# Earlier halves, moved waits, and small products placed between the halves of projection units

## The chip, the cores and the metric

The kernel runs on one core of one Trainium2 chip. The metric is the device time of one execution in microseconds, as the median of the runs shown. Five engines run their own instruction queues in order and meet at semaphores: TensorE (PE, matrix products), VectorE (DVE), ScalarE (ACT), GpSimd (POOL) and SyncE (SP, which issues the loads).

## What is computed

x is 256 tokens by 1024, in fp32. Four layers follow each other. The first two have a token mixer and a feed-forward part, with a layer norm after each; the second of them feeds forward through eight experts, two per token. The last two are of another kind:

```python
def token_mixer(x, ...):                       # first block, both layers
    q_a, k_a, v_a, x_m, z_m = split(x @ w_in)
    y_a = dilated_attention(q_a, k_a, v_a, rel_bias)
    y_m = sigmoid(z_m) * norm(mlstm(conv(x_m), x_m))
    g_a, g_m = split(sigmoid(x @ w_gate + b_gate))
    return (g_a * (y_a @ w_br_a) + g_m * (y_m @ w_br_m)) @ w_o
...
for l in range(DEPTH):                         # second block
    p = rms_norm(x) @ w_in[l]
    y_a = conformer_conv(p)                    # 31 taps over 256 channels, layer norm, silu
    y_b = head_rms_norm(moba_attention(p))     # 4 heads of 64; with 256 tokens plain causal attention
    y_c = head_rms_norm(gla_chunked(p)) * silu(p)   # 4 heads, chunks of 32, a state carried between them
    x = x + concatenate([y_a, y_b, y_c]) @ w_out[l]
    x = x + conv_swiglu(rms_norm(x))
return rms_norm(x)
```

## The kernel before

Every weight comes in units of 1 MB (128 partitions by 2048 fp32 numbers), in one order for the whole program. SP loads unit u into one of six `raw` slots when the unit six earlier has been split. ACT copies it rounded to `w_hi` and DVE writes the rest to `w_lo` (`split`, L1329 and L1738); both have three slots, so ACT waits until PE has used the unit three earlier. PE makes each product as three (`product`, L626 to L628: high by high, high by low, low by high). Activations are split in the same way (`xT_hi`, `xT_lo`).

The order on each engine is written out by hand, with `ahead(n)` for the split of unit n + 2 of the second mixer. In what follows "the low part" is DVE's half of a split. A projection unit is 48 products of 128x256; `project_tok` and `project_T` can run a function `between` their halves of 24.

- Start: ACT splits units 0 and 1, then copies the transposed x in four quarters (`x_parts`); DVE has the low parts behind it. POOL reads the shifted relative bias back from memory and loads small tables.
- First mixer's end: the gated branches are merged quarter by quarter on DVE (L2065, L2067), ACT copies them and DVE writes the low part (`low`, L2036). Five output units (`WO_UNITS`) use them; `busy_while_norm` then keeps PE at dummy products until the norm's diagonals `dg` allow `transpose_x`.
- Router and experts: DVE ranks the logits, writes `pick` (which token sits in which slot) and `extra_ready`; PE gathers the tokens (`dispatch`) and runs 14 steps per expert, each with two units up and one down. After the last expert its output is split (`expert_out`: `eo_hi`, `eo_lo`), scattered to tokens by four pairs of products, weighted into x and normed.
- Second mixer (`mixer2`, twice): units 0 to 10 are projections, 11 to 14 outputs (`w_out`). Between them stand small products: `within_chunks`, `state_steps`, `gla_out` (the memory's four heads, 36 products of 128 columns), `scores` and the attention heads (`next_pair`). 18 of the 31 taps of the convolution run on POOL, 13 on DVE (`convolve`). DVE carries the state over eight chunks in `st8` (L2330).

In the second mixer PE's order after unit 7 was:

```python
pe.wait_ge(S_.state_ready, L + 1)
gla_out((0,))
pe.wait_ge(S_.proj2_out, L * 11 + 8)
scores(0, (2, 3))
scores(1, (4, 7))
gla_out((1, 2, 3))
tok(8)
```

## Time and profile before

| what | us |
|---|---|
| median of 3 runs (2372.72 to 2376.57) | 2374.25 |
| the profiled execution | 2371.58 |
| its span, first to last instruction | 2369.8 |
| PE busy in the span | 2298.3 |
| DVE busy | 1734.5 |
| ACT busy | 1346.8 |

The span is what the trace covers; the profiled execution has 1.8 us more around it. PE is busy 97% of the span, so an idle time elsewhere matters only where PE ends up waiting for it. PE's products overlap, and their ends are modelled, so a busy PE is not always a fast one: its granted clock stands beside it.

### The profile page before, as it was taken

To read this page: it belongs to the slowest core of one execution; us is meant where nothing else is said; L and a number is where in the kernel's file an instruction comes from. 1 tells how busy PE (TensorE), PEld (TensorE's weight loads), DVE (VectorE), ACT (ScalarE), POOL (GpSimd) and SP (SyncE) were. 2 spreads that over 40 slices of the span, in tenths; PEclk is the share of its full clock that TensorE was granted. 3 is DMA by queue.
4 is the path that set the end of the run, shared out by engine and by line. 5 is a ranking of instruction groups with operands and counts; after the bars stand their busy time and mean duration, and the time that the engine had idled before them with its cause. 6 is when DMAs were issued, how large, how long until landed. Compare 5 with 4: busy or idle time off the path is not lost.

```text
span 2369.8 us, 41753 instructions
## 1 busy us (share of the span) xinstructions
PE 2298.3 (97%) x16557; PEld 2154.3 (91%) x16557; DVE 1734.5 (73%) x1853; ACT 1346.8 (57%) x1346; POOL 186.7 (8%) x181
## 2 busy tenths in 40 slices
PE   7999999999899999999999999999889999999998
PEld 7999999999799999999999999999888999898997
DVE  4556555557588888888888888888566777676776
ACT  4643433554376767676767776776336444636443
POOL 2000000100000000000000000000390000670000
PEclk9999999999999999999999999999979999999999
DMA  9344655534399999999999999999432555433551
GB/s 301 116 143 145 211 177 177 175 108 152 121 357 335 354 339 350 335 353 333 357 350 337 347 337 351 335 350 344 126 107 90 179 176 195 129 116 118 202 174 56
DMA packets 423083, 554.41 MB, mean 234 GB/s; under 512 B 9907, under 2 KB 377253, under 8 KB 422993
## 3 DMA queue, kind: packets, MB, share of 16 engines
q1 hardware_dynamic: 419232, 544.85, 68.2%
q0 software_dynamic: 3760, 8.31, 1.3%
q8 instruction: 62, 1.02, 0.2%
q14 instruction: 29, 0.23, 0.0%
HBM read 552.06 MB, written 1.06 MB: 233 GB/s over the span
## 4 chain that ended last, share of the span: by engine, by line
PE 86%; DVE 6%; ACT 3%; DVEq 2%; issue 1%; DMA 1%; ACTq 0%; SPq 0%
PE ps L626 26%; PE ps L627 26%; PE ps L628 26%; DVE w_lo L1738 2%; ACT w_hi L1329 2%; PE ps L1008 1%; PE ps L671 1%; PE ps L1025 1%; PE ps L1204 1%; DVE cvT L2238 1%; DVEq L2239 0%; DMA raw<-in_w_in 0%; PE ps L824 0%; PE ps L1202 0%; PE ps L1070 0%
## 5 line engine op out<-in xcount | busy, mean ns | idle before, releaser
L1738 DVE TENSOR_TENSOR w_lo<-raw,w_hi 128x2048 fp32r<-128x2048 f32 x519 | 1181.5, 2286 | 338.2 <-ACT w_hi L1329 336.5
L1329 ACT ACTIVATE w_hi<-raw 128x2048 fp32r<-128x2048 f32 x519 | 986.5, 1907 | 252.2 <-PE ps L628 232.1
L626 PE MATMUL ps<-w_hi,xg_hi 128*128 128x256 f32 x1792 | 516.8, 288 | 2.2 <-DVE w_lo L1738 2.2
L628 PE MATMUL ps<-w_hi,xg_lo 128*128 128x256 f32 x1792 | 504.9, 282 | 0.0
L627 PE MATMUL ps<-w_lo,xg_hi 128*128 128x256 f32 x1792 | 504.8, 282 | 0.0
L626 PE MATMUL ps<-xT_hi,w_hi 128*128 128x256 f32 (+1 forms) x1712 | 490.1, 286 | 11.0 <-DVE xT_lo L1748 6.8
L627 PE MATMUL ps<-xT_lo,w_hi 128*128 128x256 f32 (+1 forms) x1712 | 485.8, 284 | 0.0
L628 PE MATMUL ps<-xT_hi,w_lo 128*128 128x256 f32 (+1 forms) x1712 | 485.7, 284 | 0.0
L626 PEld LDWEIGHTS ps<-w_hi,xg_hi 128*128 128x128 f32 x1792 | 338.1, 189 | 9.4 <-DVE xg_lo L2150 2.9
L626 PEld LDWEIGHTS ps<-xT_hi,w_hi 128*128 128x128 f32 (+1 forms) x1712 | 328.4, 192 | 16.1 <-issue 8.9
L627 PEld LDWEIGHTS ps<-w_lo,xg_hi 128*128 128x128 f32 x1792 | 338.3, 189 | 3.8
L628 PEld LDWEIGHTS ps<-w_hi,xg_lo 128*128 128x128 f32 x1792 | 338.0, 189 | 0.0
L627 PEld LDWEIGHTS ps<-xT_lo,w_hi 128*128 128x128 f32 (+1 forms) x1712 | 328.5, 192 | 1.6
L628 PEld LDWEIGHTS ps<-xT_hi,w_lo 128*128 128x128 f32 (+1 forms) x1712 | 328.3, 192 | 0.4
L626 PE MATMUL ps<-w_hi,hT_hi 128*128 128x512 f32 x536 | 212.7, 397 | 1.0 <-DVE hT_lo L2159 1.0
L627 PE MATMUL ps<-w_lo,hT_hi 128*128 128x512 f32 x536 | 212.0, 395 | 0.0
L628 PE MATMUL ps<-w_hi,hT_lo 128*128 128x512 f32 x536 | 211.6, 395 | 0.0
L626 PE MATMUL ps<-w_hi,xT_hi 128*128 128x256 f32 (+1 forms) x448 | 130.9, 292 | 9.1 <-DVE w_lo L1738 5.5
L627 PE MATMUL ps<-w_lo,xT_hi 128*128 128x256 f32 (+1 forms) x448 | 128.7, 287 | 0.0
L628 PE MATMUL ps<-w_hi,xT_lo 128*128 128x256 f32 (+1 forms) x448 | 128.7, 287 | 0.0
L628 PEld LDWEIGHTS ps<-w_hi,hT_lo 128*128 128x128 f32 x536 | 100.8, 188 | 23.8
L1551 ACT ACTIVATE sa<-ps 128x256 f32<-128x256 f32 x112 | 43.1, 385 | 139.3 <-PE ps L628 139.1
(455 smaller groups left out, 2840.2 us busy)
## 6 DMA issues: line engine op xcount, KB each, us to landing
raw<-in_exp_w SPq DMA_DIRECT2D x336, 1024.0 KB, 5.8
raw<-in_ffn_w_up SPq DMA_DIRECT2D x44, 1024.0 KB, 5.1
raw<-in_w_in SPq DMA_DIRECT2D x42, 1024.0 KB, 6.2
raw<-in_ffn_w SPq DMA_DIRECT2D x33, 1024.0 KB, 5.1
raw<-in_ffn_w_down SPq DMA_DIRECT2D x22, 1024.0 KB, 5.5
raw<-in_w_gate SPq DMA_DIRECT2D x16, 1024.0 KB, 5.4
raw<-in_w_out SPq DMA_DIRECT2D x8, 1024.0 KB, 4.9
raw<-in_w_o SPq DMA_DIRECT2D x6, 1024.0 KB, 5.8
```

The lines of the kernel that those rows point to most:

```text
L626: pe.matmul(out, lhs[0], rhs[0], start=first, stop=False)
L627: pe.matmul(out, lhs[0], rhs[1], start=False, stop=False)
L628: return pe.matmul(out, lhs[1], rhs[0], start=False, stop=last)
L671: m = pe.matmul(o[:, c, t, :], piece, dg[:, t, :], start=True, stop=True)
L1008: m = pe.matmul(bank(0, KC, P)[:, k, :], x[:, t, k * P:(k + 1) * P], pick[:, t, :], start=t == 0, stop=t == TT - 1)
L1025: m = pe.transpose(ps[:, 7, c * P:(c + 1) * P], hf[:, 0, c * P:(c + 1) * P], ident)
L1204: m = pe.matmul(o, qgm[rows, h // 2, t, j, :], st8[rows, 4 * t + j, h // 2, :], start=False, stop=j == 3)
L1329: act.activation(w_hi[:, u.const % SPL, 0:width], raw[:, u.const % RAW, 0:width], ACT.Copy)\
L1551: act.activation(sa[:, odd, 0:FFC], ps[:, 6, 0:FFC], ACT.Silu).then_inc(S_.silue_ready, 1)
L1738: dve.tensor_tensor(w_lo[:, u.const % SPL, 0:width], raw[:, u.const % RAW, 0:width], w_hi[:, u.const % SPL, 0:width].bitcast(F32), ALU.sub ...
L2238: dve.scalar_tensor_tensor(cvT[:, c, :], avT[:, c, k:k + S], w, cvT[:, c, :], ALU.mult, ALU.add)
```

## The change

It changes orders and waits; PE's products stay the same but for 30 dummies.

- Start: unit 0 is loaded, split and used in two halves, behind the first two and the last two quarters of x; the constants are loaded after unit 3, and POOL's read of the bias waits for unit 3, the loads behind it for the convolution.
- First mixer's end: `low(0)` and `low(1)` stand together after the first pair; PE does the first halves of output units 0 and 1, then the second halves; unit 1's second tile sums in bank 4.
- Router: the split of unit 2 moves from before the ranking to after `pick`; the gates move behind step 1.
- Last expert: the output is summed, split, scattered and added half by half, in the norm's order. 120 dummies in place of 90 before the second block.
- Second mixer: PE's scores go between the halves of unit 8, two heads of `gla_out` after it, two between the halves of unit 9; the second attention pair and the first gated transposes between the halves of unit 10; the sums over channels between the halves of output units 0 and 1; output rows 3 before 1. DVE and ACT are reordered to match; unit 5's split goes ahead of the gate's logarithm.

```diff
-SUM_BANKS = ((0, 5), (1, 1), (2, 2), (3, 3), (4, 4))
+SUM_BANKS = ((0, 5), (1, 4), (2, 2), (3, 3), (4, 4))
...
-OUT2_ROWS = (2, 1, 3, 0)
-OUT2_BANKS = (1, 2, 4, 5)
+OUT2_ROWS = (2, 3, 1, 0)
+OUT2_BANKS = (1, 2, 5, 6)
...
-            sp.dma_start(cst_init[:], A["const3"]).then_inc(S_.start_loaded, 16)
-            sp.dma_start(cst1[:], A["const1"]).then_inc(S_.start_loaded, 16)
...
                 for n, c in enumerate(IN1_COLS):
+                    if (L, n) == (0, 0):
+                        for half in range(2):
+                            k = slice(4 * half, 4 * half + 4)
+                            sp.dma_start(raw[:, 0, :].rearrange("p (k n) -> p k n", k=KC)[:, k, :], columns(w_in, 256 * c, 256)[:, k, :])\
+                              .then_inc(raw_landed[0] if half else S_.half_landed, 16)
+                        continue
                     load(u + n, columns(w_in, 256 * c, 256), UW, c == 0)
+                    if (L, n) == (0, 3):
+                        sp.dma_start(cst_init[:], A["const3"]).then_inc(S_.start_loaded, 16)
+                        sp.dma_start(cst1[:], A["const1"]).then_inc(S_.start_loaded, 16)
...
-            pool.dma_start(shifted[:], bass.AP(tensor=bias_rows.tensor, offset=0, ap=[[1, P], [BUCKET_W, HA], [1, S]]))\
-                .then_inc(S_.bias_loaded, 16)
...
+                else:
+                    pool.wait_ge(raw_landed[3], 16)
+                    pool.dma_start(shifted[:], bass.AP(tensor=bias_rows.tensor, offset=0, ap=[[1, P], [BUCKET_W, HA], [1, S]]))\
+                        .then_inc(S_.bias_loaded, 16)
+                    pool.wait_ge(S_.conv1_done, 1)
                 pool.dma_start(norm_gb[:, 0, :], over(A["ln_g"][L, 0], D)).then_inc(S_.norm_loaded, 16)
...
+                if halves:
+                    pe.wait_ge(S_.lo_half, 1)
+                    w = [v[:, 0, :].rearrange("p (k n) -> p k n", k=KC) for v in (w_hi, w_lo)]
...
+                        if halves and (c, k) == (0, 4):
+                            pe.wait_ge(S_.lo_ready, RAW + 1)
...
+                def out_half(n, half, parts):
+                    c0, w = WO_UNITS[n]
+                    for t in range(TT):
+                        for k in range(4 * half, 4 * half + 4):
+                            m = product(bank(SUM_BANKS[n][t], TT, w)[:, t, :], [v[:, t * P:(t + 1) * P] for v in x_chunks[k]],
+                                        [v[:, k, :] for v in parts[n]], k == 0, k == KC - 1)
+                    if half:
+                        m.then_inc(S_.unit_used, 1)
+                pe.wait_ge(S_.xT_lo_ready, L * 12 + 6)
+                parts = [unit_parts(u + 22, KC, WO_UNITS[0][1])]
+                out_half(0, 0, parts)
+                parts.append(unit_parts(u + 23, KC, WO_UNITS[1][1]))
+                out_half(1, 0, parts)
+                pe.wait_ge(S_.xT_lo_ready, L * 12 + 8)
+                out_half(0, 1, parts)
+                out_half(1, 1, parts)
...
+                    for h in range(2):
+                        for c in range(2):
+                            m = product(ps[:, 4 + h, :], [v[:, 0, 0, c * P:(c + 1) * P] for v in (hT_hi, hT_lo)],
+                                        [v[:, c, h * HALF:(h + 1) * HALF] for v in w], False, c == 1)
+                        m.then_inc(S_.unit_used if h else S_.eo_psum, 1)
...
                 for q in range(4):
-                    scatter(q, q)
+                    if q % 2 == 0:
+                        pe.wait_ge(S_.eo_lo_ready, item.value(plus=2 + q // 2))
+                    scatter(NORM_ORDER[q], q)
...
-                busy_while_norm(6, 10 if L else 90)
+                busy_while_norm(6, 10 if L else 120)
...
-                gla_out((0,))
-                pe.wait_ge(S_.proj2_out, L * 11 + 8)
-                scores(0, (2, 3))
-                scores(1, (4, 7))
-                gla_out((1, 2, 3))
-                tok(8)
+                def both_scores():
+                    pe.wait_ge(S_.proj2_out, L * 11 + 8)
+                    scores(0, (2, 3))
+                    pe.wait_ge(S_.state_ready, L + 1)
+                    scores(1, (4, 7))
+                tok(8, both_scores)
+                gla_out((0, 1))
+                tok(9, lambda: gla_out((2, 3)))
                 next_pair = attention(L, HB, (sb0, sb1), pT2, vb, (S_.pT2_psum, S_.pT2_ready, S_.pv2), (2, 3),
                                       (ps[:, 4, 0:256], ps[:, 4, 256:512]))
                 pe.wait_ge(S_.expd2, L + 1)
                 next_pair(0)
...
-                def first_values():
+                def second_pair():
                     pe.wait_ge(S_.proj2_out, L * 11 + 9)
                     next_pair(1)
-                tok(9, first_values)
+                    gated_T(0)
+                tok(10, second_pair)
                 next_pair(2)
-                pe.wait_ge(S_.conv_ready, L + 1)
-                channel_sum(0, cvT, S_.csum_psum)
-                tok(10, lambda: gated_T(0))
-                def both_T():
+                def sum_and_T():
+                    pe.wait_ge(S_.conv_ready, L + 1)
+                    channel_sum(0, cvT, S_.csum_psum)
+                    gated_T(1)
+                def square_and_T():
                     attended_T()
-                    pe.wait_ge(S_.yT2_lo_ready, L * 4 + 1)
-                    gated_T(1)
+                    pe.wait_ge(S_.csq_ready, L + 1)
+                    channel_sum(S, agT, S_.cvar_psum)
                 bank_free(11)
-                w_out(0, yM_chunks[0:2], both_T)
-                pe.wait_ge(S_.csq_ready, L + 1)
-                channel_sum(S, agT, S_.cvar_psum)
-                w_out(1, yA_chunks[2:4])
-                w_out(2, yM_chunks[2:4])
+                w_out(0, yM_chunks[0:2], sum_and_T)
+                w_out(1, yM_chunks[2:4], square_and_T)
+                w_out(2, yA_chunks[2:4])
                 w_out(3, yA_chunks[0:2])
                 busy_while_norm(7, 10)
...
-                expert_out(at)
+                for h in range(2):
+                    if h == 0:
+                        act.wait_ge(S_.eo_psum, 1)
+                    else:
+                        used(at)
+                    act.activation(eo_hi[:, h * HALF:(h + 1) * HALF], ps[:, 4 + h, :], ACT.Copy).then_inc(S_.eo_hi_ready, 1)
...
+                ahead(3)
                 act.wait_ge(S_.glog_in, L + 1)
...
                 act.activation(egT[:], egT[:], ACT.Ln, bias=1.0).then_inc(S_.gln_ready, 1)
-                ahead(3)
                 out(3, kcT[:], bank(1, 2, S))
...
                     m.then_inc(S_.yT2_hi_ready, 1)
                 pT_pair(0)
-                ahead(9)
+                ahead(10)
                 pT_pair(1)
-                out(9, rt2[:, :, 0:256], bank(1, TT, 256), ACT.Silu)
-                ahead(10)
                 act.wait_ge(S_.yc_psum, L * 2 + 1)
-                high(yM_hi[:, 0:2, :], 3, 70)
+                high(yM_hi[:, 0:2, :], 7, 70)
+                out(10, rt2[:, :, 256:512], bank(0, TT, 256), ACT.Silu)
+                ahead(11)
+                act.wait_ge(S_.yc_psum, L * 2 + 2)
+                high(yM_hi[:, 2:4, :], 3, 72)
                 square_root(S_.sqrt2_in, S_.sqrt2_out, L * 3 + 2, stat[:, 112:120])
                 act.wait_ge(S_.cent_ready, L + 1)
                 act.activation(agT[:], cvT[:], ACT.Square).then_inc(S_.csq_ready, 1)
-                out(10, rt2[:, :, 256:512], bank(0, TT, 256), ACT.Silu)
-                ahead(11)
                 act.wait_ge(S_.yb_psum, L + 1)
                 high(yA_hi[:, 2:4, :], 0, 74)
-                act.wait_ge(S_.yc_psum, L * 2 + 2)
-                high(yM_hi[:, 2:4, :], 3, 72)
                 square_root(S_.sqrt2_in, S_.sqrt2_out, L * 3 + 3, agT[:, 0, :])
...
+                ahead(14)
                 square_roots(8 * L + 4)
                 x_parts(L * 8 + 20, 0, scale=gain(2 * L + 1))
-                ahead(14)
...
-                x_parts(L * 12, 4, beta(1) if L else None)
+                if L:
+                    x_parts(L * 12, 4, beta(1))
+                else:
+                    x_parts(0, 4, parts=(0, 1))
+                    first_half()
+                    x_parts(0, 4, parts=(2, 3))
+                    second_half()
                 split(u + 1)
...
-                            if b:
-                                low(b - 1)
+                            if b == 3:
+                                low(2)
+                        if c == 0:
+                            low(0)
+                            low(1)
...
-                split(Count(MOE_UNIT0 + 2))
-                dve.wait_ge(S_.lgT_psum, 1)
+                dve.wait_ge(S_.logits_psum, 2)
...
-                dve.wait_ge(S_.totals_psum, 1)
+                split(Count(MOE_UNIT0 + 2))
+                dve.wait_ge(S_.slots_psum, 2)
...
-                gates()
                 for j in range(1, EARLY):
                     step(Count(0), j, False)
+                    if j == 1:
+                        gates()
...
-                expert_out(item)
-                dve.wait_ge(S_.y_psum, item.value(4, 4))
-                for t in range(TT):
-                    dve.scalar_tensor_tensor(x[:, t, :], bank(2 * t, D), gate_of[:, t, bass.ds(item.value(), 1)], y_sum[:, t, :],
-                                             ALU.mult, ALU.add)
-                dve.drain()
-                for t, h in QUARTERS:
+                for h in range(2):
+                    dve.wait_ge(S_.eo_hi_ready, item.value(plus=1 + h))
+                    q = slice(h * HALF, (h + 1) * HALF)
+                    dve.tensor_tensor(eo_lo[:, q], ps[:, 4 + h, :], eo_hi[:, q].bitcast(F32), ALU.subtract).then_inc(S_.eo_lo_ready, 1)
+                for q, (t, h) in enumerate(NORM_ORDER):
+                    dve.wait_ge(S_.y_psum, item.value(4, q + 1))
+                    dve.scalar_tensor_tensor(quarter(t, h), ps[:, q, :], gate_of[:, t, bass.ds(item.value(), 1)],
+                                             y_sum[:, t, h * HALF:(h + 1) * HALF], ALU.mult, ALU.add)
+                    dve.drain()
                     half_stats(t, h)
...
                 m.then_inc(S_.glog_in, 1)
+                ahead(3)
...
                 ahead(6)
-                convolve(3)
-                ahead(7)
+                convolve(1)
...
                 m.then_inc(S_.state_ready, 1)
+                ahead(7)
+                convolve(2)
...
                 ahead(8)
+                convolve(CW - taps[0])
+                ahead(9)
...
                 gated(0)
+                dve.wait_ge(S_.conv_part_ready, L + 1)
+                dve.tensor_tensor(cvT[:], cvT[:], conv_part[:], ALU.add).then_inc(S_.conv_ready, 1)
                 ahead(10)
+                low(yM_lo[:, 0:2, :], 7, 70, yM_hi[:, 0:2, :], 1)
+                gated(1)
```

DVE at the start, before, from its last constants on (`w_lo` is the low part of a unit, `xT_lo` that of a quarter of x):

```order
L2459 MEMSET stat 128x1
L1738 TENSOR_TENSOR w_lo<-raw,w_hi 128x2048
L1925 MEMSET xmT 128x4x3
L1748 TENSOR_TENSOR xT_lo<-ps,xT_hi 128x512 x4
L1738 TENSOR_TENSOR w_lo<-raw,w_hi 128x2048 x3
L1899 TENSOR_SCALAR xcT<-xmT,cols 128x256 x4
```

and in the changed kernel:

```order
L2538 MEMSET stat 128x1
L1991 MEMSET xmT 128x4x3
L1814 TENSOR_TENSOR xT_lo<-ps,xT_hi 128x512 x2
L1802 TENSOR_TENSOR w_lo<-raw,w_hi 128x1024
L1814 TENSOR_TENSOR xT_lo<-ps,xT_hi 128x512 x2
L1808 TENSOR_TENSOR w_lo<-raw,w_hi 128x1024
L1792 TENSOR_TENSOR w_lo<-raw,w_hi 128x2048 x3
```

A whole unit stood before the four quarters; now half a unit follows each two of them.

DVE after the last expert's last unit, before (`eo_lo` the low part of its output, BN_STATS the norm's sums):

```order
L1738 TENSOR_TENSOR w_lo<-raw,w_hi 128x2048
L2164 ISA
L2165 TENSOR_TENSOR eo_lo<-ps,eo_hi 128x1024
L2213 ISA
L2215 ISA
L2215 SCALAR_TENSOR_TENSOR x<-ps,gate_of,y_sum 128x1024
L2215 ISA
L2215 SCALAR_TENSOR_TENSOR x<-ps,gate_of,y_sum 128x1024
L1865 BN_STATS stat<-x 128x6 x4
```

and in the changed kernel:

```order
L1792 TENSOR_TENSOR w_lo<-raw,w_hi 128x2048
L2289 ISA
L2291 TENSOR_TENSOR eo_lo<-ps,eo_hi 128x512
L2289 REGISTER_ALU
L2291 TENSOR_TENSOR eo_lo<-ps,eo_hi 128x512
L2293 ISA
L2294 ISA
L2294 SCALAR_TENSOR_TENSOR x<-ps,gate_of,y_sum 128x512
L1931 BN_STATS stat<-x 128x6
L2293 REGISTER_ALU
L2294 ISA
L2294 SCALAR_TENSOR_TENSOR x<-ps,gate_of,y_sum 128x512
```

The output and x are made in halves and quarters, and the statistics of a quarter follow it at once.

PE in layer 0's second mixer, before, from unit 7's last products (`kbT,qbT` are the scores, `vc,atT` and `st,qgm` the memory's heads):

```order
L627 MATMUL ps<-xT_lo,w_hi 128x256
L628 MATMUL ps<-xT_hi,w_lo 128x256
L1202 MATMUL ps<-vc,atT 128x128
L1204 MATMUL ps<-st,qgm 128x128 x3
L1202 MATMUL ps<-vc,atT 128x128
L1204 MATMUL ps<-st,qgm 128x128 x4
L1192 MATMUL ps<-kbT,qbT 128x128 x4
L1192 MATMUL ps<-kbT,qbT 128x256 x4
L1202 MATMUL ps<-vc,atT 128x128
L1204 MATMUL ps<-st,qgm 128x128 x3
```

and in the changed kernel, at the middle of unit 8:

```order
L635 MATMUL ps<-w_hi,xT_hi 128x256
L636 MATMUL ps<-w_lo,xT_hi 128x256
L637 MATMUL ps<-w_hi,xT_lo 128x256
L1225 MATMUL ps<-kbT,qbT 128x128 x4
L1225 MATMUL ps<-kbT,qbT 128x256 x4
L635 MATMUL ps<-w_hi,xT_hi 128x256
L636 MATMUL ps<-w_lo,xT_hi 128x256
```

and after unit 8, up to the first products of unit 9:

```order
L636 MATMUL ps<-w_lo,xT_hi 128x256
L637 MATMUL ps<-w_hi,xT_lo 128x256
L1235 MATMUL ps<-vc,atT 128x128
L1237 MATMUL ps<-st,qgm 128x128 x3
L1235 MATMUL ps<-vc,atT 128x128
L1237 MATMUL ps<-st,qgm 128x128 x4
L1235 MATMUL ps<-vc,atT 128x128
L1237 MATMUL ps<-st,qgm 128x128 x3
L1235 MATMUL ps<-vc,atT 128x128
L1237 MATMUL ps<-st,qgm 128x128 x4
L629 REGISTER_ALU
L635 MATMUL ps<-w_hi,xT_hi 128x256
```

The scores stood after the first head, with no unit between unit 7 and them; they now divide unit 8, and the first two heads lie between units 8 and 9.

## Rows read from the trace of the kernel before

**Rows 1.** Page: busy us (share, instructions); clock in 40 slices.

```profile
PE 2298.3 (97%) x16557; PEld 2154.3 (91%) x16557; DVE 1734.5 (73%) x1853; ACT 1346.8 (57%) x1346; POOL 186.7 (8%) x181
...
PEclk9999999999999999999999999999979999999999
```

**Rows 2.** PE's waits over the span: us in total, times, longest.

```profile
PE ps L626 <- DVE w_lo L1738: 12.0, 6, 3.3
PE ps L671 <- DVE dg L1846: 9.7, 4, 5.8
...
PE ps L1202 <- DVE st L2330: 5.2, 2, 3.5
```

**Rows 3.** Windows: length, busy us (instructions) by engine, PE clock, DMA, GB/s.

```profile
15.84:22.67 6.83, 4.21 (x20) 4.25 (x21) 5.21 (x7) 3.52 (x10) 6.83 (x9) 0.50 1.06 363
1683.97:1821.10 137.13, 129.80 (x884) 120.02 (x884) 88.20 (x160) 63.93 (x80) 77.81 (x67) 0.87 0.33 110
2027.98:2156.06 128.08, 121.70 (x884) 113.74 (x884) 91.68 (x160) 65.73 (x81) 80.29 (x68) 0.93 0.37 122
1750.84:1802.19 51.35, 46.93 (x277) 42.61 (x277) 28.70 (x84) 17.89 (x27) 24.50 (x22) 0.73 0.25 82
2097.73:2137.15 39.42, 36.84 (x277) 34.37 (x277) 28.45 (x79) 17.90 (x27) 20.53 (x19) 0.96 0.33 108
1753.22:1780.53 27.31, 26.16 (x104) 22.14 (x105) 11.09 (x33) 3.04 (x9) 22.12 (x20) 0.50 0.16 53
```

**Rows 4.** Timeline at the start, ACT, PE: start, us, instruction, idle before.

```profile
12.12 1.91 ACT L1329 ACTIVATE w_hi<-raw 128x2048 fp32r<-128x2048 f32 x1 [6.72 <-DMA raw<-in_w_in]
15.13 1.91 ACT L1329 ACTIVATE w_hi<-raw 128x2048 fp32r<-128x2048 f32 x1 [1.10 <-DMA raw<-in_w_in]
16.95 2.01 ACT L1347 ACTIVATE xT_hi<-ps 128x256 fp32r<-128x256 f32 x7
...
8.05 3.65 PE L669 MATMUL ps<-cst,x 128*128 128x128 f32 x16 [3.17 <-issue]
18.45 0.55 PE L626 MATMUL ps<-xT_hi,w_hi 128*128 128x256 f32 x1 [6.76 <-DVE xT_lo L1748]
```

**Rows 5.** Timeline at the output units of layer 0, DVE then PE.

```profile
182.01 0.69 DVE L2036 TENSOR_TENSOR xT_lo<-ga,xT_hi 128x512 fp32r<-128x512 f32 x1 [1.07 <-ACT xT_hi L1526]
...
186.18 0.69 DVE L2036 TENSOR_TENSOR xT_lo<-ga,xT_hi 128x512 fp32r<-128x512 f32 x1
...
187.01 0.36 PE L626 MATMUL ps<-w_hi,xT_hi 128*128 128x256 f32 x1 [1.81 <-DVE xT_lo L2036]
```

**Rows 6.** Timeline of PE in the first expert's second step.

```profile
649.18 0.39 PE L626 MATMUL ps<-w_hi,xg_hi 128*128 128x256 f32 x1 [2.17 <-DVE w_lo L1738]
```

**Rows 7.** Timeline after the last expert, ACT, DVE, then PE.

```profile
1661.18 1.02 ACT L1560 ACTIVATE eo_hi<-ps 128x1024 fp32r<-128x1024 f32 x1 [1.88 <-PE ps L628]
...
1667.00 2.48 DVE L2215 SCALAR_TENSOR_TENSOR x<-ps,gate_of,y_sum 128x1024 f32<-128x1024 f32 x2 [3.54 <-PE ps L1071]
1669.55 2.47 DVE L1865 BATCH_NORM_STATS2 stat<-x 128x6 f32<-128x512 f32 x4
...
1682.95 0.16 DVE L1844 RECIPROCAL stat<-stat 128x1 f32<-128x1 f32 x1 [4.01 <-DMA cst<-in_const]
...
1666.64 11.49 PE L677 MATMUL ps<-yA_hi 128*128 128x256 f32 x90
```

**Rows 8.** Chain that ended last: transposes that open the second mixers.

```profile
1683.97 5.92 PE ps L671 x32
...
2027.98 3.84 PE ps L671 x32
```

**Rows 9.** Timeline of PE: unit 5, second channel sum, last output unit.

```profile
1725.14 0.38 PE L626 MATMUL ps<-w_hi,xT_hi 128*128 128x256 f32 x1 [2.21 <-DVE w_lo L1738]
...
1808.67 0.60 PE L1231 MATMUL ps<-agT,cst 128*128 128x256 f32 x2
...
1821.10 0.49 PE L626 MATMUL ps<-w_hi,yA_hi 128*128 128x512 f32 x1 [0.48 <-DVE yA_lo L2412]
```

101 lines of the change are left out of this document (52 added, 49 removed).

## The prediction

> **What bounds the kernel now.** I read the page first: PE is busy 2298.3 of 2369.8 us, and the clock line has one slice of the last third at 7 [rows 1]. So TensorE's queue is the length of the program, and only three things can shorten it, since the change keeps its work almost unchanged: time in which PE is idle (71.5 us), work done at the lower clock level (1.2 in place of 2.4 GHz), and the tail. Then PE's waits: the largest are for `w_lo`, for the diagonals `dg` of the norms, and for `st8` [rows 2]. Then windows over the stretches at the low clock and over the two second mixers [rows 3]. Those two windows hold the same 884 PE instructions, at mean clocks 0.87 and 0.93 and in 137.1 and 128.1 us; the reader is to see that layer 0 is 9 us slower for nothing in the code. Most of that lies in one part: from the end of unit 7 to the first output unit, 277 instructions took 51.35 us in layer 0 and 39.42 in layer 1, since 27.31 us of the former ran at clock 0.50 [rows 3]. The timeline gives the rest.
>
> **1. The start.** PE's first product begins at 18.45 us, after 6.76 us of idling for `xT_lo`: ACT takes units 0 and 1 (1.91 us each, from 12.12 and 15.13, as they land) before the transposed x, which PE had ready at 11.7 [rows 4]. In the new order ACT copies two quarters of x, half a unit, two quarters, half a unit. A unit of 1 MB takes 15.13 - 12.12 = 3.0 us to land, and the 832 columns of constants now behind four units were 832/2048 of one, 1.2 us. So half 0 lands at 12.1 - 1.2 - 1.5 = 9.4 us. ACT: x quarters to 10.1 (2.01/7 = 0.29 us per copy, two per quarter), half of 1.91 to 11.1. DVE: half of its unit's 2.3 us, to 12.3. PE starts at about 12.35, and its first 12 products, at the start's slow 0.21 us each (20 in 4.21 us, [rows 3]), cover quarters 2 and 3 and the second half, whose low part is there at 14.7. **-6.1 us.** Before, the slow clock held on for 4.2 us after the first product; I take the same again. Unit 1 must be split by 20.0: landed at 13.9, ACT to 15.8, DVE to 18.1. POOL's copy of `shifted` now waits for unit 3 (about 22 us), and nine small loads behind it for the convolution (about 33); the norm needs them after 200 us, `shifted` is needed at 41. Only what is left ahead of it, `wqk` (0.8 MB, 2.3 us of the queues), can push units 1 and 2, with 2 and 4 us of room. Bounds: -4 (a late unit 1) to -8 (the clock rises early).
>
> **2. The output units, twice.** PE waits 1.81 us for `low(1)`, which DVE writes behind a split and a gating, at 186.18 [rows 5]. Written straight after `low(0)` (182.0) it ends at 183.4, before PE needs it (185.2). The second wait, for `low(3)`, moves from about 189.6 to 189.9, but PE now has the first halves of two units, 48 products (5.8 us, to 191.0), in place of 24. After that both queues are as before. 2 x 1.81: **-3.6 us**; bounds -3.6 and -2.
>
> **3. Router and first expert.** The split taken off the router's front (2.3 us) comes back between `pick` and `extra_ready`, and PE dispatches only after `extra_ready`: no gain. The gates no longer stand ahead of unit 3's split; PE's 2.17 us wait for it goes [rows 6]. But the gates' 2.7 us now come after step 1: DVE reaches the split of the next step's gating half about 0.9 us after PE could start it. **-1.3 us**; bounds -2.2 and 0.
>
> **4. The last expert and the norm after it.** Before: `eo_hi` whole (1.02), `eo_lo`, four scatters, then DVE 2.48 for x and 2.47 for the statistics, to 1672.0 [rows 7]. Now the first half is copied while PE does the second; DVE is held by its split to 1661.6, then does two halves of 0.65 to 1662.9; PE scatters from 1662.4; DVE starts on the first quarter at 1663.1 and needs 4 x (0.69 + 0.69) = 5.5 us, to 1668.6. **-3.4 us**, and all behind it follows: the norm, the load of `cst2`, which is issued after the norm and is what DVE waits for (4.01 us at 1682.95, [rows 7]); the new order leaves that wait alone. PE's idle 5.83 us before the transposes (the 9.7 of [rows 2] holds it) is covered by 30 more dummies: 120 at 11.49/90 = 0.128 us are 15.3 us, from 1664.8 to 1680.1, against `dg` at 1683.9 - 3.4 = 1680.5. So they don't delay the transposes, by only 0.4 us, and the clock should not fall: the 32 transposes took 5.92 us here and 3.84 in layer 1 [rows 8]. **-2.1 us.** Bounds for both: -6 and -3.
>
> **5. The second mixers.** PE's instructions are the same, only placed elsewhere. A mean clock of 0.87 means 0.13/0.5 x 137.13 = 35.7 us at half speed, which cost 17.8; in layer 1 17.9 us cost 9.0. So the work at full clock is 129.8 - 17.8 = 112.0 and 121.7 - 9.0 = 112.7: take 112.5 [rows 3]. To it comes what PE still waits for. I followed the new queues with durations of the same instructions:
> - Unit 5's split before the log: its waits of 2.21 us [rows 9] and, in layer 1, 3.3 [rows 2] go, and ACT and DVE are 1.7 us earlier. But PE now meets what was hidden behind unit 5: `within_chunks` needs `qkg_ready`, 1.8 us after unit 5, and unit 6 its split, 0.4 us.
> - The state steps (5.2 us of waits, [rows 2]) end at about 1748 in layer 0's clock, PE asks for them at 1752: hidden behind unit 7 and the first half of unit 8. The scores need unit 7's copy, 0.7 us after PE's end of it; hidden too.
> - Unit 9 around `gla_out` leaves ACT waiting for unit 9 with the root and the transposed heads queued behind it. The heads' values are wanted by PE after half of unit 10 (2.9 us), ACT has them 1.2 us sooner. DVE's first half of the gated output is ready 2 us before PE wants it.
> - The end: the chain from the second channel sum to `yA_lo` (split, reciprocal, Silu, two copies) took from 1809.7 to 1821.0 [rows 9]. Now only half an output unit and one whole one (8.5 us) lie over it, before there were two (11.3); against that ACT no longer waits for a unit in it (-1.3), while DVE does the `low` of attention first (+0.6). PE idles about 2.1 us, before 0.48.
> That is 112.5 + 4.3 = 116.8 us, with 1 us for about eight new hand-overs. The low clock does not vanish: it came after PE idled 2.2, 3.3 and 3.5 us, and such gaps (1.8 and 2.1) stay. I allow two stretches of 3.4 us per layer, 3.4 us lost. Total 121.2 us: layer 0 from 137.1 - 2.1 (counted in 4) saves 13.8, layer 1 6.9. **-20.7 us.** Without low clock it would be -27.5; with layer 0's long stretch as it is now, about -10.
>
> The Trainium skill (TensorE: Matmul & The Clock Gate, What's actually happening) says that the array is slow by default and activity releases it. In layer 0 the slow clock outlasted 22 us of small products, and rose in layer 1 while the same kind ran: the trace does not show that products of few rows keep it down. The Trainium skill (same page, Part 4: PE-mode transpose) says that transposes do not count as busy; by that the ones ahead of the first product don't warm the clock and step 1 is the -6.1 it is, and if the rule failed the products would start faster and step 1 would be about -8. The trace agrees so far: the first products ran at 0.21 us each behind transposes that had ended 6.8 us earlier, which doesn't decide it.
>
> Edits at nothing: `ahead(14)` before the roots on ACT (its 1.9 us lie under the last output unit, and the first square shifts by 0.2 us; without that cover the norm would be 1.9 us late); the banks and the merged semaphores, which no queue waits for anew.
>
> **Sum.** -6.1 - 3.6 - 1.3 - 5.5 - 20.7 = -37.2 us. The profiled execution took 2371.58 us, 1.8 over its span; with the change 2334.4. The median is 2374.25, 2.7 above it, so I put **2337 us**.
>
> **Rivals.**
> (a) The clock sticks again in one mixer. For: it did for 27 us, and `gla_out` is the same work. Against: each pair of heads now stands next to 24 full products. It gives back 10 to 13 us: 2349.
> (b) The POOL convolution becomes the wait. It needs 24.5 us busy in the 51 us window [rows 3] and runs slower beside DVE; it ended just before its sum is now asked for, and DVE has 2 us over before PE starves. 3 us late in both layers costs about 4: 2341.
> (c) The start is bound by transfers: the half units cost as much as whole ones, and `wqk` delays unit 1. Step 1 gives 2 instead of 6: 2341.
> (d) The mixers' order doesn't help: waits of the attention chain, now in the middle of units, take what the moved products gave. PE must then idle 20 us more than I count: 2358.
> (e) Slower than before: TensorE stays at the low clock from unit 7 to the last output unit in both layers. That stretch has 50 us of work per layer; all of it slow costs 50 per layer, against 37 gained and what is slow now (14 and 2 us lost). It decides from about 27 us extra loss per layer, as if 54 of some 60 us ran slow. Nothing ran slow that long here: about 2385.
>
> **Chances.** The forecast (2326 to 2345) 0.60, (a) 0.14, (b) or (c) 0.12, (d) 0.09, within 0.2% 0.02, (e) 0.03. Range **2326 to 2354**: below, no low clock (-6.8) and an early rise at the start; above, (a) and (d) in part. What a measurement of this kernel can tell from no change is some 0.2%, 4.7 us. Faster 0.95, same 0.02, slower 0.03.
>
> **What would show it.** PE's first product near 12.3 us; no wait of 1.8 us before the output units; the state's wait gone and one of 1 to 2 us before `within_chunks`; windows of the second mixers of 119 to 123 us each, with mean clocks of 0.93 or more; dummies touching the transposes at about 1670. Wrong would be: a new wait over 2 us on `qkg_ready`, `expd2` or `conv_ready`, dummies that end after `dg`, or a clock of 0.5 over more than 10 us in a mixer.

## The result, and the profile of the changed kernel

The changed kernel took 2338.48 us (median of 4 runs, 2336.45 to 2340.86), and before 2373.97 (median of 4). The ratio is 0.985 with an interval of 0.983 to 0.987: 35.5 us faster, where the forecast had 37 and 2337 us. The profiled execution was the slowest of the four, 2340.86 us, with a span of 2339.1; the forecast for a profiled one was 2334.4.

The page of the changed kernel, busy time of TensorE and VectorE and the granted clock in 40 slices (compare [rows 1]):

```profile
PE 2285.8 (98%) x16587; PEld 2142.9 (92%) x16587; DVE 1738.8 (74%) x1857; ACT 1344.1 (57%) x1346; POOL 191.8 (8%) x181
PEclk9999999999999999999999999999999999999999
```

TensorE is busy 12.5 us less with the same work and 30 dummies more, and the slice at 7 is gone. Its waits (engine, line, released by: us in all, times, longest):

```profile
PE ps L635 <- DVE w_lo L1792: 5.7, 5, 2.0
PE ps L686 <- DVE dg L1912: 5.5, 4, 1.7
PE ps L635 <- DVE yA_lo L2491: 5.5, 2, 2.7
PE ps L1031 <- DVE extra_sb L2193: 3.9, 1, 3.9
...
PE ps L1018 <- DVE rt L2176: 3.2, 1, 3.2
...
PE ps L635 <- DVE yM_lo L2340: 2.6, 1, 2.6
PE ps L1199 <- DVE qcT L2388: 2.5, 2, 2.2
```

Against [rows 2]: the 6.8 us for `xT_lo` at the start, the state's 5.2 and half of the 12.0 for `w_lo` are gone. New or longer are 2.7 us per layer for `yA_lo` (before 0.5), 2.6 for `yM_lo` in layer 0 (before 0.9), 3.9 for `extra_sb` (before 1.3), and 2.5 for `qcT`, which is `qkg_ready`: 2.16 us of it in layer 1.

To see where the time went, I cut both traces at the first product with `dg` of each norm, which TensorE runs in the same order in both:

| stretch | before | after | difference | forecast |
|---|---|---|---|---|
| start to the norm behind the first mixer | 219.3 | 211.3 | -8.0 | -7.9 |
| dense layer | 197.2 | 197.2 | 0 | 0 |
| first mixer, layer 1 | 199.1 | 198.2 | -0.9 | -1.8 |
| router, experts, norm | 1068.4 | 1062.2 | -6.2 | -4.7 |
| second mixer, layer 0 | 145.3 | 132.0 | -13.3 | -15.9 |
| its dense layer | 198.7 | 200.2 | +1.5 | 0 |
| second mixer, layer 1 | 136.3 | 130.9 | -5.3 | -6.9 |
| its dense layer and the end | 205.5 | 207.1 | +1.6 | 0 |

The windows show what lies behind the last four (length, busy us and instructions of PE, PEld, DVE, ACT, POOL, then the clock). After: both mixers up to the last output unit, then that unit up to the next norm's diagonals, then 6 us of the dense layer behind its wait of 2.02 us:

```profile
1668.90:1791.10 122.20, 116.16 (x883) 107.71 (x884) 89.84 (x160) 62.53 (x79) 81.33 (x67) 0.99 0.39 123
2001.04:2122.15 121.11, 115.86 (x884) 108.00 (x884) 94.24 (x160) 64.23 (x80) 82.01 (x68) 0.99 0.39 129
1791.10:1800.88 9.78, 8.51 (x35) 6.89 (x35) 5.62 (x11) 6.33 (x15) 0.00 (x0) 0.83 0.33 109
2122.15:2131.98 9.83, 8.56 (x34) 6.91 (x34) 5.59 (x11) 6.33 (x15) 0.00 (x0) 0.83 0.33 107
1825.15:1831.15 6.00, 6.00 (x37) 6.00 (x38) 5.64 (x8) 1.70 (x1) 0.00 (x0) 0.72 0.82 279
```

The same two places in the kernel before:

```profile
1821.10:1829.28 8.18, 6.91 (x34) 5.75 (x34) 5.57 (x11) 4.54 (x14) 0.00 (x0) 1.00 0.40 128
1853.56:1859.56 6.00, 6.00 (x49) 6.00 (x50) 5.64 (x8) 1.71 (x1) 0.00 (x0) 1.00 0.82 279
```

The mixers came to 122.2 and 121.1 us, forecast 121.2 each. But the last unit takes 9.8 us in place of 8.2, at clock 0.83 in place of 1.00, and 6 us of the dense layer hold 37 products in place of 49. That is 1.5 to 1.7 us at four places, and makes up the 6.5 us by which this execution missed the profiled time forecast (2334.4 us).

Two waits were new. First the sum of the convolution's parts in layer 0, VectorE (start, us, instruction, idle before), and TensorE behind it:

```profile
1763.56 0.69 DVE L2452 TENSOR_TENSOR cvT<-cvT,agT 128x512 f32<-128x512 f32 x1 [5.10 <-POOL agT L617]
1764.16 2.28 DVE L1792 TENSOR_TENSOR w_lo<-raw,w_hi 128x2048 fp32r<-128x2048 f32 x1
1766.37 0.87 DVE L2340 SCALAR_TENSOR_TENSOR yM_lo<-ps,cols,yM_hi 128x256 fp32r<-128x256 f32 x2
...
1767.48 0.49 PE L635 MATMUL ps<-w_hi,yM_hi 128*128 128x512 f32 x1 [2.60 <-DVE yM_lo L2340]
```

VectorE stood 5.1 us before GpSimd's part, with the split and `yM_lo` queued behind it. Second the end of the mixer, ACT, VectorE and TensorE:

```profile
1781.44 0.42 ACT L1419 ACTIVATE agT<-agT 128x256 f32<-128x256 f32 x1 [1.27 <-DVE agT L2484]
1781.77 3.71 ACT L1365 ACTIVATE w_hi<-raw 128x2048 fp32r<-128x2048 f32 x2
...
1788.45 1.09 ACT L1755 ACTIVATE cvT<-cvT,cols 128x256 f32<-128x256 f32 x2 [1.68 <-DVE cvT L2489]
...
1783.70 2.29 DVE L1792 TENSOR_TENSOR w_lo<-raw,w_hi 128x2048 fp32r<-128x2048 f32 x1 [2.29 <-ACT w_hi L1365]
1785.91 1.74 DVE L2487 RECIPROCAL agT<-agT 128x256 f32<-128x256 f32 x1
...
1791.10 0.49 PE L635 MATMUL ps<-w_hi,yA_hi 128*128 128x512 f32 x1 [2.73 <-DVE yA_lo L2491]
...
1791.89 0.39 PE L635 MATMUL ps<-w_hi,yA_hi 128*128 128x512 f32 x1
...
1792.46 0.63 PE L637 MATMUL ps<-w_hi,yA_lo 128*128 128x512 f32 x1
```

The root is there at 1781.9; the reciprocal that needs it starts 4 us later, behind a split that itself waits for ACT. TensorE idles 2.73 us, and 1 us after it resumes its products go from 0.39 to 0.63 us.

### The profile page after: what moved, and what is told of

It is laid out like the page before. It is cut to its first block, busy times and chain, and to the rows that moved or that the text cites. A ratio compares the mean times of both kernels' runs of the same rounds, so it can differ in the third digit from the quotient of the medians.

```text
span 2339.1 us, 41825 instructions
## 1 busy us (share of the span) xinstructions
PE 2285.8 (98%) x16587; PEld 2142.9 (92%) x16587; DVE 1738.8 (74%) x1857; ACT 1344.1 (57%) x1346; POOL 191.8 (8%) x181
## 4 chain that ended last, share of the span: by engine, by line
PE 88%; DVE 4%; ACT 2%; POOL 2%; issue 1%; DVEq 1%; POOLq 1%; ACTq 0%; DMA 0%
PE ps L635 27%; PE ps L636 26%; PE ps L637 26%; PE ps L1031 1%; POOL agT L617 1%; POOLq L616 1%; PE ps L686 1%; PE ps L1048 1%; DVE w_lo L1792 1%; ACT w_hi L1365 1%; POOL tap L611 1%; PE ps L839 0%; PE ps L1237 0%; PE ps L1102 0%; PE ps L831 0%
## 5 line engine op out<-in xcount | busy, mean ns | idle before, releaser
L635 PE MATMUL ps<-w_hi,xT_hi 128*128 128x256 f32 (+1 forms) x448 | 129.0, 288 | 0.0
```

The costliest lines, as they stand in the source:

```text
L635: pe.matmul(out, lhs[0], rhs[0], start=first, stop=False)
```

## Experiments

Each kernel was timed in up to 12 executions beside before. Four of them shared a chip (the mixers' order alone, everything but the mixers, the filled waits and the 90 dummies; before 2367.63 us, median of 24). The others shared another chip: the changed kernel again, the split behind `extra_ready`, the later sum and the root beside a before of 2372.26 (11 executions), the rest beside one of 2369.33 (17).

**The changed kernel again.** 

> The changed kernel again, beside before on one chip. On this chip's fellow, before ran from 2363 to 2385 us with mean clocks from 0.988 down to 0.977, while the mixers' new order alone stayed within 2351 to 2358. If the new order also ends the chance of a long stretch at clock 0.50, the changed kernel's runs lie within 6 us of each other and before's do not; and the gain is then 27 to 30 us against before's runs of clock 0.986 and over, 35 against those at 0.983. If before's spread is the chip's, the changed kernel spreads as widely.

Measured 2339.0 us (2336.6 to 2340.7), ratio 0.987 (0.985 to 0.989). Before ran from 2360 to 2375 beside it. I parted before's 52 executions on the two chips by their mean clock: 20 at 0.983 or less, median 2373.0 us, and 32 above, median 2366.5. No execution of the changed kernel was below 0.990. So something that happens by chance in before does not happen in it, and the gain is 27 us against one part of before and 34 against the other. None of the 52 has a trace, so that it is the long slow stretch of [rows 3] is read from the mean clocks alone.

**The mixers' order alone.** The diff's parts in the second mixers, on top of before.

> Before, with the second mixers' new order alone (TensorE, ACT, VectorE, output rows and banks); start, output units, router, last expert and dummies as before. If the steps add up, it takes 20.7 us off as step 5 has it (2353), each mixer from the transposes to the last output unit's start in 121 to 124 us. Rival: the changed kernel's mixers are fast because what stands before them (120 dummies, an earlier norm) keeps the clock up; then the order alone gives 10 us or less, and layer 0 shows a stretch of over 10 us at clock 0.50.

Measured 2353.72 us (2350.8 to 2358.2 in 10), ratio 0.993 (0.991 to 0.995). Its mixers:

```profile
1683.34:1805.53 122.19, 117.33 (x883) 109.37 (x884) 93.53 (x160) 62.41 (x79) 79.94 (x67) 0.97 0.38 123
2015.52:2135.12 119.60, 114.35 (x883) 106.50 (x884) 92.09 (x160) 64.22 (x80) 82.86 (x68) 1.00 0.40 130
```

The absolute time is the one forecast, the gain 14 us and not 20.7, since before itself was faster here. The windows belong to the order, and not to what stands ahead of it. Layer 1 ran wholly at clock 1.00: the mixer's work is 114.35 us, not 112.5.

**Everything but the mixers.**

> The changed kernel with the second mixers' order of before; all the other parts are in. By the terms of the forecast (6.1 + 3.6 + 1.3 + 5.5) it stands 16.5 us below before, about 2357.5. If the clock in layer 0's mixer depends on when it begins and not on the order, the 27 us at clock 0.50 are gone too, and it stands 25 to 28 us below (2347).

Measured 2354.12 us (ratio 0.992, 0.989 to 0.995), in two groups: 2346.0 to 2346.8 three times, 2353.0 to 2355.2 six times. The profiled one is of the second:

```profile
1668.54:1794.42 125.88, 120.64 (x884) 112.47 (x884) 91.93 (x160) 64.03 (x80) 78.95 (x67) 0.95 0.37 119
2001.33:2138.60 137.27, 130.71 (x884) 121.20 (x884) 90.48 (x160) 65.87 (x81) 80.17 (x68) 0.86 0.35 113
2074.43:2098.32 23.89, 23.89 (x99) 20.49 (x98) 10.55 (x30) 3.00 (x8) 17.21 (x16) 0.50 0.19 67
```

The same old order gives layer 0 the good window and layer 1 the 137 us one: the reverse of [rows 3]. The long slow stretch is not layer 0's; it can come in either, from the state's wait (here 1.85 us, ended 1.6 us before the stretch begins) through the small products.

**Waits filled with products of no use, before's order.** Ahead of unit 5 and ahead of memory's heads:

```
+                fill(2, 24 if L else 16)
                 tok(5)
...
+                pe.wait_ge(S_.proj2_out, L * 11 + 7)
+                fill(0, 12 if L else 26)
                 pe.wait_ge(S_.state_ready, L + 1)
```

> Before, with products of no use put into TensorE's waits of the second mixers: ahead of unit 5 (16 in layer 0, 24 in layer 1) and ahead of the first of memory's heads (26 and 12), so that these waits are busy. No wait gets shorter. If idling is what lowers the clock, the stretches at 0.50 that begin there (3.4 and 27.3 us in layer 0, 6.8 and 3.4 in layer 1) go, and 10 to 15 us with them (2359 to 2364): then half of the mixers' gain is the clock's. If the small products keep the clock low, or nothing here decides it, the time stays at 2371 to 2376.

Measured 2358.95 us, ratio 0.997 (0.9945 to 0.9994): seven executions at 2354.0 to 2359.2, five at 2367.0 to 2371.4. The profiled one, of the first group, its mixers:

```profile
1681.25:1806.34 125.09, 121.50 (x926) 113.39 (x926) 90.42 (x160) 64.14 (x80) 78.59 (x67) 0.99 0.37 120
2013.25:2138.51 125.26, 120.66 (x920) 112.22 (x920) 92.57 (x160) 65.94 (x81) 81.32 (x68) 0.99 0.39 124
```

No unit came sooner, and TensorE does 78 products more, yet the mixers take 12 and 3 us less than in [rows 3], and by the medians the kernel takes 8.7 us less. Layer 0, where no wait over 1.2 us was left idle, has no slow stretch but the end of one that began ahead of its transposes; layer 1, where 2.33 us of the state's wait stayed idle, has one of 3.4 us. So idling does lower the clock here, and the 15 us that the two mixers gain are as much as the 13.7 us that TensorE idles in them before; most of it is one long stretch, which before has only in some executions. It did not hold in every execution: by their mean clocks (0.985 to 0.988, the others 0.990 to 0.995) the five slow ones had some 27 us more at clock 0.50, an estimate. None of them has a trace, and the 2.33 us left idle in layer 1 may be what let the clock stick.

**Only the scores moved.** On TensorE alone; ACT's and VectorE's queues as before:

```
-                pe.wait_ge(S_.state_ready, L + 1)
-                gla_out((0,))
-                pe.wait_ge(S_.proj2_out, L * 11 + 8)
-                scores(0, (2, 3))
-                scores(1, (4, 7))
-                gla_out((1, 2, 3))
-                tok(8)
+                def both_scores():
+                    pe.wait_ge(S_.proj2_out, L * 11 + 8)
+                    scores(0, (2, 3))
+                    pe.wait_ge(S_.state_ready, L + 1)
+                    scores(1, (4, 7))
+
+                tok(8, both_scores)
+                gla_out((0, 1, 2, 3))
```

> Before, with one move on TensorE alone: both tiles' scores between the halves of unit 8, and all of memory's heads behind that unit. ACT's and VectorE's queues stay as they are. The wait for the state (3.5 and 1.7 us) should be hidden behind unit 7 and half of unit 8: 5 us less than before, and if the sticking of the slow clock came from that wait and the 22 us of small products in one piece, no run shows a clock of 0.98 or less. If the rest of the new order (ACT and VectorE) is needed for it, TensorE waits for expd2 or for the state instead, the time is that of before within 3 us, and some runs stick as before.

Measured 2361.08 us, ratio 0.9965 (0.995 to 0.998); 12 executions within 2359.3 to 2365.2, none at a clock below 0.986. Its waits:

```profile
PE ps L1231 <- DVE cvT L2364: 4.3, 2, 2.7
...
PE ps L1192 <- DVE st L2331: 1.7, 1, 1.7
...
PE ps L749 <- ACT pT L1672: 1.3, 1, 1.3
```

This one move ends the sticking, as far as mean clocks tell: no execution at 2370 us or over, where before beside it has 8 of 17. In layer 1 it did so with a wait as long as before's (1.75 us for the state, before 1.69), so there it seems to be the parting of the small products that counts; in layer 0 the wait of 3.53 us went too. The 5.2 us wait for the state shrinks to 1.7, but 5.6 us come up elsewhere, above all for the convolution's sum. It gives 8 us against before on its chip, the whole order 14 on the other: the rest seems to take ACT's and VectorE's new queues, which hide the sum; no run separates them.

**90 dummies for 120.**

```
-                busy_while_norm(6, 10 if L else 120)
+                busy_while_norm(6, 10 if L else 90)
```

> The changed kernel with 90 dummies ahead of layer 0's second mixer in place of 120. By the forecast's step 4 the transposes fall to clock 0.50 again after about 5 us of idling, and it costs 2.1 us against the changed kernel (2340.5). If the idle time doesn't matter for the clock there: no difference, and the 32 transposes still take 3.8 us.

Measured 2342.10 us (2339.1 to 2344.3), ratio 0.988 (0.984 to 0.991). The chain of work, first this kernel, then the changed one:

```profile
1667.86 6.75 PE ps L686 x32
```

```profile
1668.90 3.84 PE ps L686 x32
```

With 5.41 us of idling ahead the transposes ran at clock 0.50 and took 2.9 us more; with 1.65 they did not. The forecast's 2.1 is borne out in kind, a little small: the stretch from these transposes to the next norm takes 132.0 us, and 129.0 in the second profile of the changed kernel, which like this one has no wait for `yM_lo`. The totals, from two chips, neither contradict nor prove it.

**The router as it was.** Split and gates where they stood before:

```
+                split(Count(MOE_UNIT0 + 2))
                 dve.wait_ge(S_.logits_psum, 2)
...
                 m.then_inc(S_.pick_ready, 1)
-                split(Count(MOE_UNIT0 + 2))
...
+                gates()
                 for j in range(1, EARLY):
                     step(Count(0), j, False)
-                    if j == 1:
-                        gates()
```

> The changed kernel with the router's split and the gates where they stood before. By the forecast's step 3 it is 1.3 us slower than the changed kernel: the 2.2 us wait ahead of unit 3 of the first expert comes back and the 0.9 us wait after it goes. The traces suggest 1.7 us more, since the changed kernel also lost a stretch of 3.4 us at clock 0.50 there: 2.5 to 3 us slower if that stretch comes back with the wait, 1.3 if it does not.

Measured 2343.06 us, ratio 0.988 (0.986 to 0.990). The stretch from the norm before the router to the next takes 1064.8 us, in the two profiles of the changed kernel 1062.2 and 1061.7: 2.6 to 3.1 us. The median is 4.1 us above the changed kernel's, with ranges that overlap. The wait that comes back:

```profile
639.91 0.39 PE L635 MATMUL ps<-w_hi,xg_hi 128*128 128x256 f32 x1 [2.14 <-DVE w_lo L1792]
```

1.1 us behind it a stretch of 3.4 us at clock 0.50 begins, as in before; the changed kernel, with 0.93 us of wait there, has none.

**The router's split behind `extra_ready`.**

```
                 m.then_inc(S_.pick_ready, 1)
-                split(Count(MOE_UNIT0 + 2))
...
                 dve.tensor_scalar(extra_sb[:], stat[0:1, 102:103], float(P), 1.0, ALU.is_gt, ALU.mult).then_inc(S_.extra_ready, 1)
+                split(Count(MOE_UNIT0 + 2))
```

> The changed kernel, with the split that the change put between pick and extra_ready placed behind extra_ready, where VectorE idled 4.2 us. TensorE's dispatch waits for extra_ready, so it should begin 2.3 us sooner (its wait falls from 3.6 to 3.9 us to about 1.4) and the kernel be 2.3 us shorter. If the first expert's tokens or weights are what is late, the 2.3 us turn up as another wait before step 1: 0.

Measured 2336.31 us (2334.4 to 2337.5), ratio 0.986 (0.983 to 0.988), 2.7 us under the changed kernel beside it, with overlapping ranges; the same stretch from norm to norm takes 1059.2 us, 2.5 to 3.0 less. The dispatch, here and in the changed kernel:

```profile
620.58 5.46 PE L1031 MATMUL ps<-pick,x 128*128 128x128 f32 x32 [1.36 <-DVE extra_sb L2192]
```

```profile
622.29 6.67 PE L1031 MATMUL ps<-pick,x 128*128 128x128 f32 x32 [3.92 <-DVE extra_sb L2193]
```

The changed kernel took the split out of one serial wait (5.3 to 3.2 us) and put it into the next (1.35 to 3.9), as step 3 read it. Behind `extra_ready` it brings no new wait.

**The convolution's sum later.**

```
-                dve.wait_ge(S_.conv_part_ready, L + 1)
-                dve.tensor_tensor(cvT[:], cvT[:], conv_part[:], ALU.add).then_inc(S_.conv_ready, 1)
                 ahead(10)
                 low(yM_lo[:, 0:2, :], 7, 70, yM_hi[:, 0:2, :], 1)
+                dve.wait_ge(S_.conv_part_ready, L + 1)
+                dve.tensor_tensor(cvT[:], cvT[:], conv_part[:], ALU.add).then_inc(S_.conv_ready, 1)
```

> The changed kernel, with VectorE's sum of the convolution's two parts placed behind the split of the last-but-one output unit and the low part of yM, instead of ahead of them. In layer 0 VectorE waited 5.10 us there for GpSimd's part and TensorE then 2.60 us for yM_lo. If that is the cause, the 2.60 us wait goes and with it a stretch of 3.4 us at clock 0.50: 2.6 to 4.3 us less than the changed kernel; layer 1 the same as it is. If the split or ACT's copy is late anyway, TensorE waits as long for w_lo or yM_lo as before: 0.

Measured 2337.11 us (2334.6 to 2337.7), 1.9 below the changed kernel, with the ranges overlapping. Its VectorE:

```profile
1760.59 0.87 DVE L2340 SCALAR_TENSOR_TENSOR yM_lo<-ps,cols,yM_hi 128x256 fp32r<-128x256 f32 x2
1763.84 0.69 DVE L2454 TENSOR_TENSOR cvT<-cvT,agT 128x512 f32<-128x512 f32 x1 [2.37 <-POOL agT L617]
```

`yM_lo` is ready 3 us before TensorE wants it, and the wait is gone. The gain is below the 2.6 expected at least, since the changed kernel beside it was without that wait in its own profile: VectorE stood only 2.00 us before the sum there. GpSimd was no faster in it: the sum starts 94.6 us after the mixer's first transposes, and 94.7 us in the profile with the wait. TensorE was late instead, after 6.83 us at clock 0.50 from 1722.51 on. Seven kept profiles have VectorE's new order with the sum where it was: in the four with the wait of 2.6 to 2.7 us no slow stretch lies between unit 5 and the sum, in the three without it one of 3.4 or 6.8 us does. So in some executions a slow stretch of TensorE hides GpSimd's part.

**The root ahead of the split.**

```
-                ahead(12)
                 dve.wait_ge(S_.sqrt2_out, L * 3 + 3)
                 dve.reciprocal(agT[:, 0, :], agT[:, 0, :])
                 dve.drain()
                 dve.tensor_tensor(cvT[:], cvT[:], spread(agT[:, 0, :], 1, 2), ALU.mult).then_inc(S_.cnorm_ready, 1)
+                ahead(12)
```

and on ACT `ahead(13)` from ahead of the Silu to behind `yA_hi`.

> The changed kernel, with the convolution norm's reciprocal and product placed ahead of VectorE's split of the last output unit, and ACT's Silu and copy ahead of its split of the unit after it. The wait of 2.73 us for yA_lo, once per layer, should fall to 0 to 0.9 us, so 3.6 to 5.5 us less, and up to 1.7 us more per layer if the clock no longer falls behind it: 4 to 9 us in all. If the split of the last unit is then what is late (w_lo), the wait stays at 1.5 us or more and the gain is 2.5 us at most.

Measured 2328.20 us (2325.5 to 2329.3), ratio 0.982 (0.980 to 0.985), 10.8 below the changed kernel beside it. Its VectorE:

```profile
1781.81 1.75 DVE L2486 RECIPROCAL agT<-agT 128x256 f32<-128x256 f32 x1 [0.48 <-ACT agT L1419]
1783.63 0.69 DVE L2488 TENSOR_TENSOR cvT<-cvT,agT 128x512 f32<-128x512 f32 x1
1784.24 2.29 DVE L1792 TENSOR_TENSOR w_lo<-raw,w_hi 128x2048 fp32r<-128x2048 f32 x1
```

The `yA_lo` wait is gone in both layers. By stretch, against the first profile of the changed kernel: the mixers with their last units 127.4 and 126.0 us (132.0, 130.9), the dense layer 198.7 (200.2). So 5.5 us of waits removed brought nearly 11: the rest is the clock that no longer falls, in this profile also a whole wait further on (1.5 us in each dense layer). That part isn't sure to be the edit's: with all three edits the `yA_lo` wait is gone as well, and the dense layers of that profile, the slowest of five executions, take 200.1 and 207.1 us again.

**All three edits, and with the waits that are left filled.** The three diffs above together; then also:

```
+                fill(2, 23)
                 pe.wait_ge(S_.chosen_ready, 1)
...
+                    fill(2, 9)
                     pe.wait_ge(S_.extra_ready, 1)
...
+                fill(2, 14 if L else 2)
                 within_chunks()
```

> The changed kernel with the three later edits together: the convolution's sum later, the root ahead of the split, the router's split behind extra_ready. Taken alone they gave 1.9, 10.8 and 2.7 us against the changed kernel on one chip. If they are independent, 15 us less than the changed kernel (2339.0 there), about 2324, with no wait for yM_lo and yA_lo in either layer. If they took the same idle time, or one shifts a wait to the next unit, 11 us or less.

> The kernel with the three edits, and products of no use in the waits that are left: 23 ahead of the router's wait for the chosen experts, 9 ahead of extra_ready, 2 and 14 ahead of within_chunks in layers 0 and 1. No wait gets shorter. If idling lowers the clock, the 10.2 us at clock 0.50 at the router (where the 32 dispatch products take 6.7 us) go or shrink, and the 3.4 us behind within_chunks in layer 1 go: 3 to 6 us less than the kernel with the three edits. If the router's small products themselves keep the clock low, 0 to 1 us less.

The three edits: 2320.82 us (2320.3 to 2327.2), ratio **0.980** (0.977 to 0.982), 18 us below the changed kernel on that chip and 48 below before. They add up, and to more than the 15.4 us that they gave one by one; why is open. With fills: 2321.33 us (2320.3 to 2322.8). The clock is a little higher (0.995 to 0.997, without 0.992 to 0.996) and the dispatch takes 5.46 us, but that it already did with the split moved alone. The expected 3 to 6 us are not there. By the two profiles the fills moved the slow clock as much as they removed it: at the router the stretch at 0.50 shrinks from 6.83 to 3.41 us, but in layer 1 one of 6.83 us stands behind the filled wait, where there were 3.41 without. The spread is narrower, 2.5 us against 6.8, with five executions each.

## Why the forecast held, step by step

- **Start.** The first product began at 12.32 us, forecast 12.35. The slow products that the forecast expected behind it came in some executions only. The changed kernel's first profile, then its second (the changed kernel again):

```profile
12.32 0.39 PE L635 MATMUL ps<-xT_hi,w_hi 128*128 128x256 f32 x1 [1.49 <-DVE w_lo L1802]
12.54 0.28 PE L636 MATMUL ps<-xT_lo,w_hi 128*128 128x256 f32 x1
...
12.32:16.32 4.00, 3.37 (x26) 3.17 (x27) 3.29 (x4) 2.64 (x2) 4.00 (x6) 1.00 1.10 348
```

```profile
12.22 0.58 PE L635 MATMUL ps<-xT_hi,w_hi 128*128 128x256 f32 x1 [1.25 <-DVE w_lo L1802]
12.60 0.41 PE L636 MATMUL ps<-xT_lo,w_hi 128*128 128x256 f32 x1
12.81 0.41 PE L637 MATMUL ps<-xT_hi,w_lo 128*128 128x256 f32 x1
...
12.32:16.32 4.00, 4.00 (x21) 4.00 (x21) 3.31 (x4) 2.54 (x3) 4.00 (x7) 1.00 1.10 347
```

- **Output units.** Both waits of 1.81 us are gone. Layer 0 gained the 1.8 in full; layer 1 0.9, with a slow stretch of 3.4 us at 478 us; in the two profiles of later runs without that stretch (the later sum, the 90 dummies) this part takes 197.1 us, 2.0 less than before.
- **Router.** -1.3 was too small: by the router put back, 2.6 to 3.1. The waits were read rightly, the 1.7 us of clock behind the 2.17 us wait was not priced.
- **Last expert and norm.** From TensorE's wait for the last `hT_lo` to `dg`: 25.9 us before (1658.1 to 1684.0), 22.4 after (1646.5 to 1668.9), so -3.5 against -3.4. The dummies ended 1.65 us ahead of `dg`, forecast 0.4: 120 took 14.54 us, 0.121 each, while the 0.128 was read where the clock was low for a part.
- **Second mixers.** 122.2 and 121.1 us against 121.2, with terms that err both ways: work 114.4 in place of 112.5 (I had taken a slow stretch to cost exactly half, and so subtracted too much), idling 6.0 and 5.3 us in place of 5.3, the slow clock 1.7 us or so in place of 3.4. The `qkg_ready` wait was 2.16 us in layer 1, forecast 1.8, and over the 2 us that the forecast itself had named as a sign of being wrong; it cost little. The forecast also tied the slow clock to waits of 2.2, 3.3 and 3.5 us alone, but [rows 3]'s layer 1 has 6.83 us at 0.50 from 2087.73 on with no wait before it, and 3.41 behind the wait of 1.69. The term that failed is the end: 2.7 us of idling for 2.1, and behind it a slow last unit and a slow dense layer that the sum left out, 6.3 us in the profiled execution.
- **Rivals.** (b) held in part, 2.6 us in layer 0 and in some executions; (a) did not occur: no profile with the new order has more than 6.83 us at clock 0.50 in one piece in a mixer, and no mean clock suggests it in the other executions; nothing spoke for (c), (d) or (e).
- **The baseline, and luck.** The -20.7 us were read off one execution of before with a 27 us stretch at clock 0.50. The runs timed then were as slow, but only 20 of 52 later ones had so low a clock; in the later runs the same order gained 14. Before's four first timings all lay there, at 2372.7 to 2376.6 us; whether by chance or by their chip is open, for the forecast it was luck. So is that the median came within 1.5 us: 2.7 us were added since before's profiled execution lay that far below its median, the changed kernel's lay 2.4 above, and the two hide most of the 6.5 us missed.

## What to carry to other kernels

Price a wait of TensorE of about 2 us or more as its length and, in most cases, some 1.7 us of slow clock behind it (half of a stretch of 3.4 us), and look for that cost in the next stage too. Where a long slow stretch makes up half of an expected gain, look at several executions of the kernel before. And when splits of weights share a queue with a serial chain, put each split behind the step that the chain waits for: here two such moves gave 2.7 and 10.8 us more alone, and 18 us together with a sum moved behind the split that it held up.
